# A decoder step on one core: the down projection in 47 passes instead of 40, with its operands made over three units

## Chip, core and metric

The kernel runs on one core of one Trainium2 chip. The metric is device time in microseconds of a whole execution; lower is better. A profiled execution also has a span, from its first to its last instruction.

## What is computed

One layer of a hybrid decoder on 512 prompt tokens and 8 x 8 sample tokens, 576 tokens in all, in float32: a mixer (gated linear attention and a state-space branch with a shared input and output projection), and behind it a feed-forward part. The change is in the latter:

```
def _conv_ffn(xn, s_ffn, p):
    u = xn @ p['ffn_w_in']                                  # 2048 -> 2 x 5632
    u, buf = _causal_dwconv(u, s_ffn, p['ffn_conv_w'], p['ffn_conv_b'])
    a, b = jnp.split(u, 2, axis=-1)
    return (jax.nn.silu(a) * b) @ p['ffn_w_out'], buf       # 5632 -> 2048
# in _layer:
x = x + _rmsnorm(f, p['n_ffn_post'])
```

## The kernel before, in words

Activations lie with channels on the 128 partitions and the 576 tokens along the free axis, in two halves of 288. A float32 product is made of three matmuls: operands are split into a high part (ScalarE copies to the rounded type) and a low part (VectorE subtracts), and high x high, high x low and low x high are added in PSUM (`three`, L1880 to L1882). On top of that, most of the feed-forward part multiplies 2 x 2 blocks by a scheme with seven products in place of eight, so sums of weight blocks and sums of activation blocks are needed, each split in two as well.

**Units.** The matrix work is an ordered stream of units. A unit is one block of 512 KB of weights (`raw`, two buffers, loaded by SP in order) and, in the down projection, two steps of seven products of three matmuls, 42 matmuls. Units are counted here from the start of the down projection: unit 0 is the loop's w = WUNITS (160), unit -1 the last of the up projection; a group of four up units gives one pair of tiles of gate input. For each unit ScalarE makes the high parts (`hi_a` L1069, `hi_s` L1079) and VectorE the sums (L2502, L2509, L2516) and the low parts (`direct_lows` L2527, `sum_lows` L2534). ScalarE may start on a unit two ahead of TensorE; the operand ring has three slots.

**The down projection.** K, the 44 gate tiles g (5632 channels), is cut into 21 pairs of tiles and two tiles for a tail. Each pair kp is loaded back from DRAM (`g_spill`) by SP (`kp_load` L573), VectorE forms its four sums in three steps (`g_first`, `g_second`, `g_third`: L2749, L2756, L2763), ScalarE makes the high parts of all seven (`g_highs` L1205, 128x2016), VectorE the low parts (`g_lows` L2769, 128x2016). There are five slots for pairs (G_SLOTS), so a pair can be loaded only when the pair five before has had its last use (`freed`, L511). The output is 8 pairs of tiles j. WINDOWS (L78) cuts the 21 pairs of each j into windows, and a pass (r, j) is window r of output pair j: in it TensorE accumulates seven products in seven of the eight PSUM banks over its steps. The 40 passes have 168 steps in 84 units. The passes of round 0 are copied to the arena by ScalarE (`take_pass` L1213, L1225). The later ones, except the last two, are staged: ScalarE copies each bank to the one buffer `m_stage`, and POOL adds it to the arena by two accumulating DMAs (L668), of products 0 to 3 and 4 to 6; the next staged pass waits for each half's DMA before it is copied. TensorE's next pass may use bank q + 1 only when product q of the last pass has been copied. The last two passes are added from PSUM by VectorE (L2786).

**The order on each engine** is fixed by one loop over w (ScalarE L1292, VectorE L2884, SP L589). `g_made_at` (L519) gives the unit in whose iteration a pair is made, with sums, high parts and low parts in the same iteration; `combined_at` (L523) the iteration in which the seven products of an output pair are combined to tiles (`combine` L2788, L2797 to L2804). SP loads a pair when its slot's last unit is done, three iterations behind in its own order, ahead of the next raw block in the same queue; `h_load` (L585) brings the residual back in the same way (10 tiles, then 6).

**The end.** A tail of 32 tile halves of six matmuls (`last_down` L1948) adds the last two tiles of K, VectorE takes them (`take_last` L2925), ScalarE squares them, the sums of squares go through TensorE (L1980, L1988), and VectorE and POOL scale (`y_of` L2931), add the residual and give the rows to the output DMAs.

The core of what sets the order, before:

```
WINDOWS = ((2, 5, 5, 5, 4),) * 4 + ((3, 5, 5, 5, 3),) * 2 + ((4, 5, 5, 4, 3), (5, 5, 5, 3, 3))
g_made_at = {WUNITS - 2: 0, WUNITS - 1: 1, WUNITS + 2: 2, WUNITS + 5: 3, WUNITS + 7: 4}
for _kp in range(5, DOWN_KP):
    g_made_at[max(freed(_kp) + 2, max(g_made_at) + 1)] = _kp
```

This puts pairs 0 to 20 in units -2, -1, 2, 5, 7, 11, 12, 21, 26, 28, 31, 32, 41, 46, 48, 51, 52, 61, 66, 68 and 70.

## Time and profile before

| | |
|---|---|
| median of 3 runs | 2566.02 us (2564.46 to 2573.86) |
| the profiled execution's own time | 2566.72 us |
| its span | 2564.9 us |
| TensorE matmuls, busy | 2462.2 us, 96% of the span |
| VectorE, busy | 1837.9 us, 72% |
| ScalarE, busy | 1080.8 us, 42% |
| POOL, busy | 444.8 us, 17% |
| mean granted TensorE clock | 0.983 |
| the chain that ended last, by engine | TensorE 76%, VectorE 11%, DMA 5%, ScalarE 4% |

Busy times are of the span. The execution's own time lies 1.8 us above its span, and 0.7 us above the median of the three runs. Matmuls overlap in the pipeline, so a matmul's duration in a row is longer than the time from one to the next; the latter is what a stretch costs. The granted clock is a share of TensorE's 2.4 GHz: 1.00 is that level and 0.50 is 1.2 GHz, and a stretch in between had some time at each. "issue" as a releaser means that the profile shows nothing that the instruction waited for.

### The profile page before, as it was taken

What the parts mean: (1) busy time and instruction counts of PE and PEld (TensorE: products, weight loads), DVE (VectorE), ACT (ScalarE), POOL (GpSimd) and SP (SyncE); (2) the same over time, 40 slices, a digit from 0 to 9 for tenths busy, and PEclk for the clock granted to TensorE, in tenths of its full rate; (3) what the DMA queues carried; (4) which work ended last, traced back from release to release, by engine and by line L of the source; (5) the groups of instructions that cost most, each with busy time, mean ns of one, the idle gap of its engine ahead of it and who ended that gap; (6) DMA issues with size and microseconds to landing.
All of it is one profiled execution on the core that took longest, in us unless ns stands there. A gap on an engine that the chain in (4) does not pass through costs nothing.

```text
span 2564.9 us, 48674 instructions
## 1 busy us (share of the span) xinstructions
PE 2462.2 (96%) x20078; PEld 2423.8 (94%) x20078; DVE 1837.9 (72%) x2763; ACT 1080.8 (42%) x1653; POOL 444.8 (17%) x268
## 2 busy tenths in 40 slices
PE   7999999999999999999999999999999899999986
PEld 7999999999999999899999999999998898989986
DVE  6543555755236368898888888988888767676778
ACT  5332222433213245444444444444445545545542
POOL 3333223433233361000000000000000011111115
PEclk9999999999999999999999999999999999999998
DMA  5223237622472424233333333333334367676883
GB/s 178 83 82 96 77 121 260 211 75 72 136 255 82 156 68 143 86 112 107 108 108 111 107 111 113 112 103 106 111 106 145 102 159 184 162 184 157 200 209 119
DMA packets 106284, 334.29 MB, mean 130 GB/s; under 512 B 11344, under 2 KB 16080, under 8 KB 105184
## 3 DMA queue, kind: packets, MB, share of 16 engines
q1 hardware_dynamic: 66400, 229.53, 28.1%
q10 hardware_dynamic: 31040, 70.90, 7.7%
q0 software_dynamic: 8640, 30.97, 6.7%
q8 instruction: 149, 2.44, 0.4%
q14 instruction: 55, 0.45, 0.1%
HBM read 255.77 MB, written 44.62 MB: 117 GB/s over the span
## 4 chain that ended last, share of the span: by engine, by line
PE 76%; DVE 11%; DMA 5%; ACT 4%; issue 3%; SPq 0%; POOL 0%; ACTq 0%; DVEq 0%
PE psum_proj L1379 18%; PE psum_proj L1381 9%; PE psum_proj L1880 7%; PE psum_proj L1882 7%; PE psum_proj L1881 7%; PE psum_work L1880 7%; PE psum_work L1882 7%; PE psum_work L1881 7%; DMA raw<-in_weights_dram 4%; PE psum_work L1379 1%; ACT ops_a L1205 1%; DVE w_lo L2534 1%; DVE w_lo L2527 1%; PE psum_work L1381 1%; DVE arena L2450 1%
## 5 line engine op out<-in xcount | busy, mean ns | idle before, releaser
L1379 PE MATMUL psum_proj<-x_hi,w_hi 128*128 128x288 f32 (+2 forms) x1696 | 510.9, 301 | 15.0 <-DVE x_lo L2031 12.9
L1379 PE MATMUL psum_proj<-x_lo,w_hi 128*128 128x288 f32 (+2 forms) x1696 | 501.2, 296 | 0.0
L1381 PE MATMUL psum_proj<-x_hi,w_lo 128*128 128x288 f32 (+2 forms) x1696 | 500.8, 295 | 0.0
L613 POOL TENSOR_TENSOR w_lo<-raw,w_hi 128x1024 fp32r<-128x1024 f32 x128 | 321.7, 2515 | 619.6 <-ACT w_hi L707 619.6
L707 ACT ACTIVATE w_hi<-raw 128x1024 fp32r<-128x1024 f32 x138 | 145.3, 1056 | 486.5 <-PE psum_proj L1381 412.0
L1379 PEld LDWEIGHTS psum_proj<-x_hi,w_hi 128*128 128x128 f32 x1696 | 320.7, 189 | 22.2 <-issue 15.4
L1379 PEld LDWEIGHTS psum_proj<-x_lo,w_hi 128*128 128x128 f32 x1696 | 320.0, 189 | 2.7 <-issue 1.9
L1381 PEld LDWEIGHTS psum_proj<-x_hi,w_lo 128*128 128x128 f32 x1696 | 319.7, 188 | 0.0
L668 POOL DMA_DIRECT2D arena<-m_stage x60 | 51.9, 868 | 1456.8 <-ACT m_stage L1225 1455.0
L1880 PE MATMUL psum_proj<-ops_a,w_hi 128*128 128x288 f32 x808 | 245.3, 304 | 29.9 <-issue 10.6
L1880 PE MATMUL psum_work<-ops_a,w_hi 128*128 128x288 f32 x782 | 234.8, 300 | 16.7 <-issue 13.0
L1882 PE MATMUL psum_proj<-ops_a,w_lo 128*128 128x288 f32 x808 | 242.3, 300 | 0.0
L1882 PE MATMUL psum_work<-ops_a,w_lo 128*128 128x288 f32 x782 | 233.6, 299 | 0.0
L1881 PE MATMUL psum_proj<-ops_a,w_hi 128*128 128x288 f32 x738 | 221.9, 301 | 0.0
L1881 PE MATMUL psum_work<-ops_a,w_hi 128*128 128x288 f32 x712 | 213.4, 300 | 0.0
L1077 ACT ACTIVATE w_hi<-raw 128x768 fp32r<-128x768 f32 x162 | 136.9, 845 | 141.0 <-PE psum_work L1882 60.3
L1880 PEld LDWEIGHTS psum_proj<-ops_a,w_hi 128*128 128x128 f32 x808 | 156.0, 193 | 35.1 <-issue 15.9
L1880 PEld LDWEIGHTS psum_work<-ops_a,w_hi 128*128 128x128 f32 x782 | 150.5, 192 | 18.4 <-issue 13.8
L2527 DVE TENSOR_TENSOR w_lo<-raw,w_hi 128x768 fp32r<-128x768 f32 x162 | 154.6, 954 | 15.5 <-ACT w_hi L1077 15.4
L1882 PEld LDWEIGHTS psum_proj<-ops_a,w_lo 128*128 128x128 f32 x808 | 156.4, 194 | 0.0
L1082 ACT ACTIVATE w_hi<-tail 128x1024 fp32r<-128x1024 f32 x81 | 86.1, 1063 | 156.5 <-DVE tail L2516 156.5
L1882 PEld LDWEIGHTS psum_work<-ops_a,w_lo 128*128 128x128 f32 x782 | 150.7, 193 | 0.0
(452 smaller groups left out, 6786.6 us busy)
## 6 DMA issues: line engine op xcount, KB each, us to landing
raw<-in_weights_dram SPq DMA_DIRECT2D x386, 512.0 KB, 3.6
arena<-m_stage POOLq DMA_DIRECT2D x30, 576.0 KB, 5.2
arena<-m_stage POOLq DMA_DIRECT2D x30, 432.0 KB, 7.2
g_spill<-x_flat ACTq DMA_DIRECT2D x44, 288.0 KB, 2.1
x_flat<-g_spill SPq DMA_DIRECT2D x18, 576.0 KB, 5.1
spill<-tail ACTq DMA_DIRECT2D x24, 288.0 KB, 2.1
arena<-in_xT_dram SPq DMA_DIRECT2D x4, 1152.0 KB, 10.6
y_spill<-arena ACTq DMA_DIRECT2D x4, 1152.0 KB, 4.9
```

Of the source, the lines that this page charges most:

```text
L613: nc.gpsimd.tensor_tensor(w_lo[:, slot], raw[:, r], w_hi[:, slot].bitcast(F32), ALU.subtract).then_inc(lo_ready, 1)
L668: pool.dma_start(m_of(j, first, stop), m_stage[:, first * HALF:stop * HALF], accum_op=ALU.add)\
L707: nc.scalar.activation(w_hi[:, slot], raw[:, r], ACT.Copy).then_inc(hi_ready, 1)
L1077: nc.scalar.activation(w_slot(w, 0)[:, 0:6], raw[:, w % 2, 2:8], ACT.Copy).then_inc(hi_ready, 1)
L1082: nc.scalar.activation(w_slot(w, 0)[:, 6:14], w_sums[w % 2], ACT.Copy).then_inc(whs_ready, 1)
L1205: nc.scalar.activation(g_high_part(kp), g_sums(kp), ACT.Copy).then_inc(op_high, 1)
L1379: nc.tensor.matmul(banks[:, n, 0:b - a], w_hi[:, slot, k], (hi, lo)[part][:, a:b], start=first and part == 0, stop=False)
L1381: mm = nc.tensor.matmul(banks[:, n, 0:b - a], w_lo[:, slot, k], hi[:, a:b], start=False, stop=last)
L1880: nc.tensor.matmul(to, w_h, hi, start=first, stop=False)
L1881: nc.tensor.matmul(to, w_h, lo, start=False, stop=False)
L1882: return nc.tensor.matmul(to, w_l, hi, start=False, stop=last)
L2527: tt_op(w_slot(w, 1)[:, 0:6], raw[:, w % 2, 2:8], w_slot(w, 0)[:, 0:6].bitcast(F32), ALU.subtract)\
```

## The change

The windows of the eight output pairs are cut anew, into 47 passes of at most five steps (six rounds; output pair 7 ends in round 4), so the last uses of the k pairs are spread over the units. Round 0 still has 8 passes; 37 passes are staged in place of 30. The 168 steps and 84 units stay. The passes of output pair 7 are over early, and its two tiles (14, 15) are the first of the tail (LAST_TILES); the combining of output pairs 4, 5 and 6 stands in the tail in place of 6 and 7.

Making a pair is spread over three iterations: sums and high parts in iteration `made`, the low parts in two instructions (4/7 and 3/7 of the columns) in the next two, each behind the lows of the unit's own weights. Pairs 0 to 20 now have their sums in units -8, -2, 3, 6, 9, 12, 15, 18, 21, 25, 31, 37, 40, 43, 46, 49, 55, 60, 63, 66 and 69. Pair 0's sums are formed in `m_stage`, which is not used before round 1; its high parts come in unit -4 and its low parts in -3 and -2; pair 1 has both low parts in -1, pair 2 both in 4. The residual's load moves from iteration 79 to 78 and the tail tiles' load from 72 to 73.

```diff
@@ -75,8 +75,10 @@
 
 
 DOWN_KP, DOWN_PAIRS = FT // 2 - 1, KT // 2
-WINDOWS = ((2, 5, 5, 5, 4),) * 4 + ((3, 5, 5, 5, 3),) * 2 + ((4, 5, 5, 4, 3), (5, 5, 5, 3, 3))
-PASSES = [(r, j, sum(WINDOWS[j][:r]), sum(WINDOWS[j][:r + 1])) for r in range(5) for j in range(DOWN_PAIRS)]
+WINDOWS = ((2, 3, 4, 3, 5, 4), (2, 3, 5, 3, 4, 4), (2, 3, 4, 5, 4, 3), (2, 4, 4, 5, 3, 3), (3, 4, 4, 4, 3, 3),
+           (3, 3, 5, 4, 3, 3), (4, 4, 3, 5, 3, 2), (4, 4, 4, 4, 5))
+PASSES = [(r, j, sum(WINDOWS[j][:r]), sum(WINDOWS[j][:r + 1])) for r in range(6) for j in range(DOWN_PAIRS)
+          if r < len(WINDOWS[j])]
 STEPS = [(p, kp) for p, (r, j, first, stop) in enumerate(PASSES) for kp in range(first, stop)]
 FIRST_STEP = [sum(q < p for q, kp in STEPS) for p in range(len(PASSES))]
 END_STEP = [sum(q <= p for q, kp in STEPS) - 1 for p in range(len(PASSES))]
@@ -87,6 +89,9 @@
 TAIL_UNITS = 4
 UNITS = TAIL_UNIT0 + TAIL_UNITS
 G_SLOTS = 5
+
+LAST_PASS = [max(p for p, (r, i, first, stop) in enumerate(PASSES) if i == j) for j in range(DOWN_PAIRS)]
+LAST_TILES = (14, 15) + tuple(range(14))
 
 BY_VE = (len(PASSES) - 2, len(PASSES) - 1)
 STAGED = [p for p, (r, j, first, stop) in enumerate(PASSES) if r and p not in BY_VE]
@@ -363,7 +368,7 @@
         def g_sums(kp):
 
             at = 4032 * (kp % G_SLOTS) + 2016
-            return smalls[:, 0:2016] if kp % G_SLOTS == 4 else XF[:, at:at + 2016]
+            return m_stage[:] if kp == 0 else smalls[:, 0:2016] if kp % G_SLOTS == 4 else XF[:, at:at + 2016]
 
         def g_tail(q, low):
 
@@ -375,8 +380,8 @@
         h_in = XF[:, 6336:6336 + KT * T].rearrange("p (n t) -> p n t", n=KT)
         H_FIRST = 10
 
-        fsum, fsum_v = A(0, 576), A(2016, 576)
-        fsq = [A(2016 * (2 + i), 576) for i in range(4)]
+        fsum, fsum_v = A(2016 * 7, 576), A(0, 576)
+        fsq = [A(2016 * (1 + i), 576) for i in range(3)] + [w_sum_b[:, 0:576]]
 
 
         const_in = sem("const_in")
@@ -510,18 +515,26 @@
 
         def freed(kp):
 
+            if kp == 0:
+                return WUNITS - 14
             if kp < 4:
                 return WUNITS - 4 + kp // 2
             if kp == 4:
                 return WUNITS + 2
             return WUNITS + LAST_USE[kp - G_SLOTS] // 2
 
-        g_made_at = {WUNITS - 2: 0, WUNITS - 1: 1, WUNITS + 2: 2, WUNITS + 5: 3, WUNITS + 7: 4}
+        made = [WUNITS - 8, WUNITS - 2, WUNITS + 3, WUNITS + 6, WUNITS + 9]
         for _kp in range(5, DOWN_KP):
-            g_made_at[max(freed(_kp) + 2, max(g_made_at) + 1)] = _kp
+            made.append(max(freed(_kp) + 2, made[-1] + 3))
+        g_made_at = {w: kp for kp, w in enumerate(made)}
+        g_high_at = {(w if kp else WUNITS - 4): kp for kp, w in enumerate(made)}
+        g_low_at = {WUNITS - 3: ((0, 0),), WUNITS - 2: ((0, 1),), WUNITS - 1: ((1, 0), (1, 1))}
+        g_low_at[made[2] + 1] = ((2, 0), (2, 1))
+        for _kp in range(3, DOWN_KP):
+            for _half in range(2):
+                g_low_at[made[_kp] + 1 + _half] = ((_kp, _half),)
         TAIL_FREED, H_FREED = (WUNITS + LAST_USE[kp] // 2 for kp in (16, 17))
-        combined_at = {WUNITS + END_STEP[p] // 2 + 2: j for p, (r, j, first, stop) in enumerate(PASSES)
-                       if r == 4 and p not in BY_VE}
+        combined_at = {WUNITS + END_STEP[p] // 2 + 3: j for j, p in enumerate(LAST_PASS) if p not in BY_VE}
 
         L = BATCHES - LATE_B
 
@@ -680,8 +693,8 @@
             def add_h(n, kt):
 
                 pool.wait_ge(y_m, KT * n + kt + 1)
-                a = cut(acc(kt), n)
-                nc.gpsimd.tensor_tensor(a, a, cut(h_in[:, kt ^ 1], n), ALU.add).then_inc(added_p, 1)
+                a = cut(acc(LAST_TILES[kt]), n)
+                nc.gpsimd.tensor_tensor(a, a, cut(h_in[:, LAST_TILES[kt] ^ 1], n), ALU.add).then_inc(added_p, 1)
 
             for kt in POOL_SUMS:
                 square_sum(0, kt)
@@ -1202,6 +1215,8 @@
             def g_highs(kp):
 
                 act.wait_ge(op_sum, KP + kp + 1)
+                if kp == 0:
+                    act.wait_ge(units_done, DOWN_UNIT0 - 3)
                 nc.scalar.activation(g_high_part(kp), g_sums(kp), ACT.Copy).then_inc(op_high, 1)
 
             def g_tail_highs():
@@ -1220,8 +1235,8 @@
                     else:
                         to = m_stage[:, M_AT[q] * HALF:(M_AT[q] + 1) * HALF]
                         before = STAGED.index(p)
-                        if before and q in (0, M_SPLIT):
-                            act.wait_ge(m_acc[q // M_SPLIT], 16 * before)
+                        if q in (0, M_SPLIT):
+                            act.wait_ge(*((m_acc[q // M_SPLIT], 16 * before) if before else (op_low, G_OPS0 + 1)))
                     nc.scalar.activation(to, bank(7 * p + q), ACT.Copy).then_inc(part_out, 1)
 
             def hi_tail(v):
@@ -1317,8 +1332,8 @@
                     g_out(g - 1)
                 if step + 1 in END_STEP and END_STEP.index(step + 1) not in BY_VE:
                     take_pass(END_STEP.index(step + 1))
-                if w in g_made_at:
-                    g_highs(g_made_at[w])
+                if w in g_high_at:
+                    g_highs(g_high_at[w])
                 if w == TAIL_FREED + 3:
                     g_tail_highs()
                 if w >= ALL_UNITS - 2:
@@ -1341,7 +1356,7 @@
                         act.wait_ge(ysq_sum, len(POOL_SUMS) * n + POOL_SUMS.index(max(kt - 4, 1)) + 1)
                     elif kt > 4:
                         act.wait_ge(ysq_vsum, len(VE_SUMS) * n + VE_SUMS.index(max(kt - 4, 5)) + 1)
-                    nc.scalar.activation(cut(fsq[kt % 4], n), cut(acc(kt), n), ACT.Square).then_inc(squared, 1)
+                    nc.scalar.activation(cut(fsq[kt % 4], n), cut(acc(LAST_TILES[kt]), n), ACT.Square).then_inc(squared, 1)
                     if n and kt == 2:
                         act.wait_ge(fo_st, 16)
                         root_of_tokens(0)
@@ -1352,8 +1367,8 @@
                 by_ve = sum(kt < stop for kt in VE_ADDS[n])
                 act.wait_ge(added_v, len(VE_ADDS[0]) * n + by_ve)
                 act.wait_ge(added_p, 2 * KT + (KT - len(VE_ADDS[0])) * n + stop - by_ve)
-                i, a = divmod(first, 4)
-                act.dma_start(yT[i, :, a:a + 2, n * HALF:(n + 1) * HALF], acc_rows(first, n)).then_inc(y_st, 16)
+                i, a = divmod(LAST_TILES[first], 4)
+                act.dma_start(yT[i, :, a:a + 2, n * HALF:(n + 1) * HALF], acc_rows(LAST_TILES[first], n)).then_inc(y_st, 16)
 
             for n in range(2):
                 for first in range(0, KT, 2):
@@ -2762,11 +2777,14 @@
                 ve.wait_ge(own_step, second_step)
                 tt_op(f[G4], f[G21], f[G2], ALU.add).then_inc(op_sum, 1)
 
-            def g_lows(kp):
+            def g_lows(kp, half):
 
                 ve.wait_ge(op_high, G_OPS0 + kp + 1)
                 ve.wait_ge(op_sum, KP + kp + 1)
-                tt_op(g_low_part(kp), g_sums(kp), g_high_part(kp).bitcast(F32), ALU.subtract).then_inc(op_low, 1)
+                a, z = ((0, 4 * HALF), (4 * HALF, 7 * HALF))[half]
+                low = tt_op(g_low_part(kp)[:, a:z], g_sums(kp)[:, a:z], g_high_part(kp)[:, a:z].bitcast(F32), ALU.subtract)
+                if half:
+                    low.then_inc(op_low, 1)
 
             def g_tail_lows():
 
@@ -2787,7 +2805,7 @@
 
             def combine(j):
 
-                p = 4 * DOWN_PAIRS + j
+                p = LAST_PASS[j]
                 m = m_of(j).rearrange("p (n t) -> p n t", n=7)
                 if p in BY_VE:
                     ve.wait_ge(*product_out(p, 6))
@@ -2893,6 +2911,8 @@
                     take_pass(END_STEP.index(step))
                 if w + 1 < ALL_UNITS:
                     sum_lows(w + 1)
+                for low_kp, half in g_low_at.get(w, ()):
+                    g_lows(low_kp, half)
                 if kp is not None:
                     g_first_step = g_first(kp)
                 if w + 2 < ALL_UNITS:
@@ -2911,21 +2931,20 @@
                     gate_product(g - 1)
                 if u == 3 and w < WUNITS:
                     evacuate(g)
+                if step + 1 in END_STEP[:-1] and END_STEP.index(step + 1) in BY_VE:
+                    take_pass(END_STEP.index(step + 1))
                 if w in combined_at:
                     combine(combined_at[w])
-                if kp is not None:
-                    g_lows(kp)
                 if w == TAIL_FREED + 3:
                     g_tail_lows()
                 if w >= ALL_UNITS - 2:
                     tail_lows(w - ALL_UNITS + 2)
-            combine(6)
             take_pass(BY_VE[1])
 
             def take_last(e):
 
                 ve.wait_ge(tile_mm, LAST_MM0 + e + 1)
-                a = cut(acc(e % KT), e // KT)
+                a = cut(acc(LAST_TILES[e % KT]), e // KT)
                 tt_op(a, last_bank(e), a, ALU.add).then_inc(taken, 1)
 
             def y_of(n, kt):
@@ -2934,11 +2953,11 @@
                     ve.wait_ge(ysq_mm, 2 * n + 2)
                     ve.wait_ge(h_back, 32)
                     ve.wait_ge(squared, Y_SQUARES0 + KT * (n + 1))
-                a = cut(acc(kt), n)
-                stt(a, a, V("ffn_post", kt), work[:, n, 0:HALF], ALU.mult, ALU.mult).then_inc(y_m, 1)
+                a, d = cut(acc(LAST_TILES[kt]), n), LAST_TILES[kt]
+                stt(a, a, V("ffn_post", d), work[:, n, 0:HALF], ALU.mult, ALU.mult).then_inc(y_m, 1)
                 if kt in VE_ADDS[n]:
                     ve.wait_ge(y_m, KT * n + kt + 1)
-                    tt_op(a, a, cut(h_in[:, kt ^ 1], n), ALU.add).then_inc(added_v, 1)
+                    tt_op(a, a, cut(h_in[:, d ^ 1], n), ALU.add).then_inc(added_v, 1)
 
             def square_sum(n, kt):
 
@@ -2952,10 +2971,10 @@
             settle()
             for e in range(2 * KT):
                 take_last(e)
-                if e in (1, 5):
-                    tail_lows(2 + e // 4)
-                if e == 3:
-                    combine(7)
+                if e in (1, 6):
+                    tail_lows(2 + e // 5)
+                if e in (3, 5, 8):
+                    combine((4, 5, 6)[e // 3 - (e == 3)])
                     settle()
                 n, kt = divmod(e - 1, KT)
                 if kt in VE_SUMS:
@@ -2996,7 +3015,7 @@
     down = f_out.reshape(FT, P, KT, P).transpose(2, 0, 1, 3)
     blocks = [[down[2 * PASSES[p][1] + n, 2 * kp + 1 - o] for o, n in ((0, 1), (0, 0), (1, 0), (1, 1))] for p, kp in STEPS]
     blocks = np.array(blocks).reshape(DOWN_UNITS, 2, 4, P, P).transpose(0, 3, 2, 1, 4).reshape(-1, P, 8, P)
-    tail = down[:, 2 * DOWN_KP:].reshape(-1, 8, P, P).transpose(0, 2, 1, 3)
+    tail = down[list(LAST_TILES), 2 * DOWN_KP:].reshape(-1, 8, P, P).transpose(0, 2, 1, 3)
 
     out = w_out.reshape(2, 8, P, KT, P).transpose(0, 3, 2, 1, 4)[::-1]
     out = np.concatenate([out[:, 8:], out[:, :8]], axis=1).reshape(-1, P, 8, P)
```

## Rows read from the trace of the kernel before

**Rows 1.** Stretches: us, then busy PE, PEld, DVE, ACT, POOL; clock, DMA share, GB/s

```profile
1959.70:2507.70 548.00, 494.30 (x3528) 487.31 (x3529) 389.39 (x556) 274.62 (x462) 51.88 (x60) 0.95 0.63 165
1959.70:1978.20 18.50, 12.84 (x64) 11.94 (x65) 18.29 (x31) 9.45 (x17) 0.00 (x0) 0.72 0.25 79
2048.90:2065.60 16.70, 11.19 (x66) 10.74 (x65) 13.90 (x18) 5.80 (x9) 0.00 (x0) 0.80 0.23 64
2065.60:2141.10 75.50, 75.50 (x568) 75.30 (x568) 49.09 (x71) 40.48 (x69) 10.51 (x12) 1.00 0.73 184
...
2176.80:2192.00 15.20, 11.15 (x65) 10.72 (x65) 12.26 (x18) 5.40 (x8) 0.00 (x0) 0.78 0.31 82
...
2462.20:2482.70 20.50, 10.65 (x65) 10.21 (x64) 10.18 (x17) 7.57 (x17) 2.34 (x3) 0.75 0.81 256
...
2507.70:2564.90 57.20, 37.17 (x254) 35.04 (x252) 46.98 (x104) 17.39 (x39) 34.78 (x40) 0.81 0.38 128
```

**Rows 2.** TensorE's waits, 1950 to 2565 us: total, times, longest

```profile
PE psum_proj L1880 <- DVE ops_a L2769: 12.3, 4, 3.8
```

**Rows 3.** TensorE in order of time: start, us, what [idle before <-releaser]

```profile
1962.80 0.37 PE L1880 MATMUL psum_proj<-ops_a,w_hi 128*128 128x288 f32 x1 [3.14 <-DVE w_lo L2534]
...
2053.54 0.37 PE L1880 MATMUL psum_proj<-ops_a,w_hi 128*128 128x288 f32 x1 [1.71 <-issue]
...
2060.35 0.61 PE L1880 MATMUL psum_proj<-ops_a,w_hi 128*128 128x288 f32 x1 [3.80 <-DVE ops_a L2769]
```

**Rows 4.** VectorE in order of time, two units that each make a pair

```profile
2048.57 2.26 DVE L2769 TENSOR_TENSOR ops_a<-x_flat,ops_a 128x2016 fp32r<-128x2016 f32 x1 [2.54 <-ACT ops_a L1205]
2050.74 0.95 DVE L2527 TENSOR_TENSOR w_lo<-raw,w_hi 128x768 fp32r<-128x768 f32 x1
...
2053.35 0.75 DVE L2749 TENSOR_TENSOR x_flat<-x_flat 128x576 f32<-128x576 f32 x1
2054.02 0.42 DVE L2509 TENSOR_TENSOR tail<-tail,raw 128x256 f32<-128x256 f32 x1
2054.35 0.45 DVE L2756 TENSOR_TENSOR x_flat<-x_flat 128x288 f32<-128x288 f32 x1
...
2058.04 2.26 DVE L2769 TENSOR_TENSOR ops_a<-x_flat,ops_a 128x2016 fp32r<-128x2016 f32 x1 [2.53 <-ACT ops_a L1205]
```

**Rows 5.** VectorE in order of time, the last up units and unit 0

```profile
1935.54 0.46 DVE L2696 TENSOR_TENSOR x_flat<-psum_proj,smalls 128x288 f32<-128x288 f32 x1 [1.78 <-ACT smalls L1155]
...
1950.86 0.69 DVE L2502 TENSOR_TENSOR tail<-raw 128x512 f32<-128x512 f32 x1 [1.74 <-DMA raw<-in_weights_dram]
...
1957.83 2.26 DVE L2769 TENSOR_TENSOR ops_a<-x_flat,ops_a 128x2016 fp32r<-128x2016 f32 x1 [2.32 <-ACT ops_a L1205]
...
1964.69 0.45 DVE L2696 TENSOR_TENSOR x_flat<-psum_proj,smalls 128x288 f32<-128x288 f32 x1
```

**Rows 6.** DMA queues and issues, 2040 to 2520 us: share; KB, us to landing

```profile
q0 software_dynamic: 8640, 30.97, 36.0%
q1 hardware_dynamic: 16956, 52.84, 31.9%
...
arena<-m_stage POOLq DMA_DIRECT2D x30, 432.0 KB, 7.2
...
x_flat<-h_spill SPq DMA_DIRECT2D x1, 2880.0 KB, 15.7
```

**Rows 7.** ScalarE's waits, 1960 to 2520 us: total, times, longest

```profile
ACT m_stage L1225 <- DMA arena<-m_stage: 0.4, 1, 0.4
```

**Rows 8.** The accumulating DMAs of L668, all 60

```profile
DMA to landing us min/median/max: 4.8/6.1/11.5
```

**Rows 9.** VectorE in order of time, behind the residual's load

```profile
2476.14 0.69 DVE L2502 TENSOR_TENSOR tail<-raw 128x512 f32<-128x512 f32 x1 [10.14 <-DMA raw<-in_weights_dram]
```

**Rows 10.** VectorE in order of time, behind the loop

```profile
2506.51 0.75 DVE L2797 TENSOR_TENSOR arena<-arena 128x576 f32<-128x576 f32 x1
...
2509.33 0.81 DVE L2786 TENSOR_TENSOR arena<-psum_proj,arena 128x288 f32<-128x288 f32 x2
```

## The prediction

> **What bounds the kernel now.** The page comes first: TensorE is busy nearly throughout, and the chain that ended last runs mostly through it, so the question is where TensorE loses time in the stage that the change touches. The table by stretch answers it [rows 1]. In the stall-free stretch of 75.5 us 568 matmuls ran, 0.133 us each at a granted clock of 1.00. The down projection, from 1959.7 to 2507.7 us, has 84 units of 42 matmuls, the 3528 that its row counts; at 0.133 they need 469 us, and it took 548. So 79 us are lost there at a mean clock of 0.95: 54 as idle time (548.0 less the 494.3 that it was busy) and the rest as matmuls at the 1.2 GHz level after idle time.
>
> The table of waits and TensorE's gaps in order of time say where [rows 2, 3]. Three gaps of 3.8 us (one stands in the rows, the others are at 2187 and 2313 us) are put down to the low parts of a k pair (VectorE, L2769), each behind a unit that began with a gap with no releaser ("issue", as before 2053.54 us). VectorE's order of work shows why [rows 4]. A unit's own operands cost it 3.3 us. A k pair adds its sums, 1.4 us, and the low parts, 2.17 us from start to start, but between the two VectorE waits 2.53 us for ScalarE's high parts, which come only when the sums are there. From one low part to the next, in two units that both make a pair, pass 9.47 us, where TensorE uses 5.58 a unit. One such unit eats the lead that VectorE has; two in a row stop TensorE twice. Late sums also hold ScalarE in its queue, so the eviction of a finished pass starts late, and TensorE stops before the next pass's second product.
>
> By loss (stretch less matmuls x 0.133): the start 10 us (18.5 less 64); pairs 5 and 6, the first double make, 7.9 us (16.7 less 66), pairs 10 and 11 6.6 (15.2 less 65), pairs 15 and 16 about as much, 20.7 together; the load of the residual 11.9 us (20.5 less 65) [rows 1]; 36.5 us are left for the single makes and late evictions.
>
> **The parts of the change.**
> *Operands over three units, makes at least three units apart.* A make unit now costs VectorE 3.3 + 1.4 = 4.7 us, the next 3.3 + 1.3, the third 3.3 + 1.0: 13.7 us (with 0.1 for a second instruction) against 3 x 5.58 = 16.7. The 2.53 us wait goes, unless ScalarE sits in the eviction of a pass; it then ends about 2.3 us into the next unit, where VectorE still has some 3 us of lead. The three double makes and the single ones should stop stalling: 20.7 + 36.5 us at most. I keep 6 us back for pairs whose first use is one unit after the last low part, or in that unit (2, 3, 4, 13, 14, 20; for pair 3 I get 0.5 us to spare), and 2 us for units 37, 46 and 55, where a make, a late weight load and a pass with an odd last step meet. **Gain 49 us.**
>
> *First pair early.* Pair 0's sums go to unit -8, its high parts to -4, the low parts to -3 and -2; pair 1 is formed at -2 and finished at -1 behind the unit's own lows. Now VectorE waits until 1957.83 us, splits pair 0 until 1960.0, and only then makes unit 0's lows; TensorE gets them at 1962.80 after 3.14 us, and the last up tile is taken at 1964.69 [rows 3, 5]. After, unit 0's lows can be done by 1958.3, before TensorE asks at 1959.7, pair 1's lows by 1960.6, and the tile is taken from about 1961.5: TensorE waits 1.5 us at its third product and follows the takes. The 10 us become 4. What is moved costs 1.4 us in group -8 and 2.2 us in -3 and -2, covered by VectorE's waits in those groups, 1.78 us for part 0's copy and 1.74 us for raw weights [rows 5]; the second wait shrinks with only one pair's load ahead of it, and that pays for it. Without the cover it would cost 2 us. **Gain 6 us.**
>
> *47 passes.* TensorE's matmuls stay 3528. Seven more staged passes are 49 more evictions on ScalarE, which is busy for 274.6 of the 548 us [rows 1] and does them beside TensorE, and 14 more accumulating DMAs on POOL's queue. Their queue held the 16 engines for 36.0% of 480 us, 173 us or 5.8 a pass; the loads took 31.9%, 153 us [rows 6]. After, it is 37 x 5.8 + 153 = 368 us against 72 units x 5.58 = 402 of TensorE: 92% full where before it was 68%. With passes of three steps (8.4 us, 13 of them behind a staged pass) a half must land before the next pass is evicted: landing of the second half 7.2 after its issue [rows 6] and 1.2 for the last evictions is 8.4, with 1.5 us of slack by the spare PSUM bank; under load it is more. I take 4 us: the trace of before shows one such wait, 0.4 us [rows 7], but it has few passes so short. Bounds: 0, if the landing stays; and 80 if it is always the longest, 11.5 [rows 8] (the rival below); I stay near the lower end, by the row of 0.4. **Cost 4 us.**
>
> The Trainium skill ("DMA: Bandwidth & Descriptors", section "Anatomy of one DMA — SWDGE (gpsimd) path") prices such a DMA at about 2.0 us plus its bytes at 436 GB/s, by which a pass would hold the engines for an estimated 2.4 us, leave them near half empty, and make the 4 us zero. The measured 5.8 us decides.
>
> *The residual's load* keeps its form: 2880 KB, 15.7 us to landing [rows 6], go ahead of the raw weights in SP's queue, now before unit 78 instead of 79, and VectorE waited 10.14 us for those weights [rows 9]. I leave its 11.9 us; bounds 9 and 15, as more accumulations share the engines.
>
> *The end.* Passes 45 and 46 are taken by VectorE. Before, the combining of two pairs of tiles stood behind the loop (2.8 us, from 2506.51 to 2509.33 [rows 10]), now that of three (4, 5, 6), while the last pass is taken some 1.7 us earlier. VectorE is busy for 47.0 of the last 57.2 us, TensorE for 37.2 [rows 1], so one more combining of 2.8 us, less what the earlier take gives back, plus the order of tiles: **cost 3.5 us**, bounds 0 (if TensorE's later gaps cover it) and 5.
>
> **Sum.** 49 + 6 - 4 - 3.5 = 47.5 us off the profiled execution's 2566.72 gives 2519; its median twin is 2566.02, 0.7 lower, so **2518.5 us**.
>
> **Rivals.**
> *The DMA engines become the bound* (faster, but by half). For it: 92% full, and in the stretches of three-step passes with a pair's load 5.8 + 1.5 x 1.5 + 1.7 = 9.8 us of transfers stand against 8.4 of TensorE. Raw weights then land late for every unit. Against: in the stall-free stretch they were 73% busy [rows 1] without harm, and the two raw buffers allow a landing of 7.4 us (two units, 11.2, less 3.8 of issue and VectorE's work between). Price: 1.4 us in each of 13 short passes and a raw landing too late at the 16 pair loads by 0.5 is 26 us, of which 4 are counted: about 2541. The Trainium skill ("DMA: Bandwidth & Descriptors", section "Queues, rings and completion order") says that an engine serves its queues in turn by packets: a raw load is then slowed beside an accumulation and not held behind it. That bears on how late, not on whether, and no row of before isolates it.
>
> *Deadlines too near.* Pairs 2, 3, 4, 13, 14 and 20 miss their first use as the double makes do now, a gap of 3.8 and 2.5 at the slow clock each: 6 x 6.3 less the 6 kept back = 32 us worse: 2550. For it: the slack is one unit or none. Against: VectorE's lead in quiet stretches is more than a unit.
>
> *Slower: the one stage buffer.* ScalarE may not evict a pass until the halves of the last one have landed. If the second half lands in 11.5 us throughout, a cycle is 12.7 us: 13 three-step passes lose 4.3 each and 16 of four steps 1.5 each, 80 us, and ScalarE, stuck there, delays the weight sums too. This passes the gain from a landing of about 10.5 us on (before: median 6.1 over both halves [rows 8]), and would give 2566 - 51.5 + 80 = 2594.
>
> *It does not do what it says*: the stalls come from the weights alone, and the makes only coincide: within 10 us of 2566. Against: the gaps end with L2769 [rows 3] and VectorE waits before it for ScalarE alone [rows 4].
>
> **How the numbers follow.** Forecast 0.64 (own range 2506 to 2532), DMA bound 0.18 (2532 to 2550), deadlines 0.09, stage buffer 0.04, no effect 0.05. 0.5% is 12.8 us, about what a measurement here can tell: the limit is 2553. Faster: 0.64 + 0.18 + 0.07 (most of the deadlines' case) = 0.89, plus 0.02 of the last two cases: 0.91. Slower 0.03, same 0.06. The low end takes every bound at its best (evictions and end at 0, 5 of the 8 us kept back, and 3 at the residual's load), 2503; the high end reaches through the DMA case, 2543.
>
> **What would show it.** Right: no gap put down to L2769; VectorE's idle time before it small; 84 units in about 492 us; the granted clock of that stretch 0.98 or more; TensorE's first product of the down projection without a wait for L2534; one long gap, about 9 us, at unit 78; DMA share near 0.75 over the stage. Wrong: gaps released by ScalarE's m_stage copies that themselves waited for the accumulating DMA (stage buffer), waits of VectorE for raw weights in most units with gaps marked "issue" (DMA bound), gaps at pairs 2, 3, 4 (deadlines). If the stretch from the last down unit to the end grows by more than 5 us, the price of the end was wrong.

## The result, and the profile after

The changed kernel takes **2550.71 us** (median of 9 runs, 2546.99 to 2558.79) against 2570.03 for the kernel before in the same job (9 runs, 2564.46 to 2573.86): ratio 0.9926, 95% interval 0.9913 to 0.9938. It is faster by 19 us, where 47.5 were forecast, and it lies 8 us above the end of the range. The profiled execution took 2550.71 us, span 2548.9.

The same stretches in the changed kernel's trace (columns as in [rows 1]): the down projection, its first 17 us, the place of unit 38, and the tail.

```profile
1957.01:2484.75 527.74, 488.19 (x3529) 480.58 (x3528) 378.29 (x562) 291.21 (x511) 63.93 (x74) 0.97 0.73 184
1957.01:1974.20 17.19, 14.74 (x95) 13.81 (x94) 16.95 (x30) 10.64 (x24) 0.00 (x0) 0.90 0.35 121
2176.80:2192.00 15.20, 11.31 (x69) 10.87 (x68) 7.34 (x11) 6.50 (x11) 1.72 (x2) 0.82 0.69 208
...
2484.75:2548.90 64.15, 38.01 (x260) 35.64 (x258) 53.44 (x111) 17.17 (x39) 34.10 (x40) 0.84 0.35 118
```

The down projection went from 548.0 us to 527.7, where the forecast's own terms give 497 (548 - 49 - 6 + 4; its list of signs says 492), and the tail from 57.2 to 64.2. The up projection ends 2.7 us earlier in this execution, which belongs to neither and is likely of this execution: in three of the kernels below that share this up projection the down projection starts at 1959.0, 1960.4 and 1961.3 us, against 1957.0 here and 1959.7 before.

Waits of the changed kernel from 1957 to 2549 us (total, times, longest), TensorE's, then ScalarE's, then VectorE's:

```profile
PE psum_proj L1895 <- ACT m_stage L1240: 12.7, 9, 2.4
PE psum_work L1895 <- ACT m_stage L1240: 10.6, 10, 2.4
PE psum_work L1895 <- issue: 10.1, 2, 9.5
...
PE psum_proj L1895 <- issue: 3.2, 2, 1.7
...
ACT w_hi L1090 <- DMA raw<-in_weights_dram: 74.2, 17, 12.5
...
ACT m_stage L1240 <- DMA arena<-m_stage: 10.3, 8, 2.1
...
DVE w_sum_b L2517 <- DMA raw<-in_weights_dram: 97.3, 21, 14.8
DVE tail L2517 <- DMA raw<-in_weights_dram: 32.9, 11, 5.9
DVE ops_a L2785 <- ACT ops_a L1220: 6.9, 4, 2.6
```

What stands in the place of the last line in the kernel before, 1957 to 2565 us:

```profile
DVE ops_a L2769 <- ACT ops_a L1205: 45.3, 16, 5.6
```

[Rows 2] has no line of its kind any more: TensorE waits nowhere for the low parts of a pair, and VectorE's waits for ScalarE's high parts, the longest item of its list before, are short. In their place stand 23.3 us of gaps, 19 of them, each ended by ScalarE's copy of a finished pass into the stage buffer (L1240), and the waits for raw weights about doubled: VectorE's from 71 to 130 us, ScalarE's (L1090; L1077 before) from 43 to 88. ScalarE also waits for the accumulating DMAs before it may refill the stage buffer, 10.3 us in 8 waits where [rows 7] had 0.4 in one.

The DMA part of the trace, 2040 to 2500 us, as in [rows 6]:

```profile
q0 software_dynamic: 10422, 37.29, 46.5%
q1 hardware_dynamic: 16471, 51.09, 30.8%
...
raw<-in_weights_dram SPq DMA_DIRECT2D x70, 512.0 KB, 6.0
arena<-m_stage POOLq DMA_DIRECT2D x36, 576.0 KB, 5.5
arena<-m_stage POOLq DMA_DIRECT2D x36, 432.0 KB, 7.9
x_flat<-g_spill SPq DMA_DIRECT2D x12, 576.0 KB, 7.1
```

The accumulations' share rose from 36.0% to 46.5%. Their own landing hardly moved (432 KB: 7.2 to 7.9 us), but a load of raw weights now takes 6.0 us to land at the median, where it took 4.1 before in the same window.

How a late load reaches TensorE shows at unit 38. In order of time: the issues of SyncE (SP), then VectorE, ScalarE and TensorE.

```profile
2164.51 0.33 SPq L606 DMA_DIRECT2D raw<-in_weights_dram  x1
2171.99 0.38 SPq L595 DMA_DIRECT2D x_flat<-g_spill  x1
2172.49 2.14 SPq L606 DMA_DIRECT2D raw<-in_weights_dram  x1
2177.56 0.38 SPq L595 DMA_DIRECT2D x_flat<-g_spill  x1
...
2170.67 0.95 DVE L2542 TENSOR_TENSOR w_lo<-raw,w_hi 128x768 fp32r<-128x768 f32 x1
...
2182.64 0.69 DVE L2517 TENSOR_TENSOR w_sum_b<-raw 128x512 f32<-128x512 f32 x1 [7.61 <-DMA raw<-in_weights_dram]
2183.26 1.22 DVE L2549 TENSOR_TENSOR w_third<-tail,w_third 128x1024 fp32r<-128x1024 f32 x1
...
2186.22 1.06 ACT L1095 ACTIVATE w_hi<-w_sum_b 128x1024 fp32r<-128x1024 f32 x1 [2.73 <-DVE w_sum_b L2531]
2187.18 0.39 ACT L1240 ACTIVATE m_stage<-psum_proj 128x288 f32<-128x288 f32 x1
...
2184.58 0.37 PE L1895 MATMUL psum_proj<-ops_a,w_third 128*128 128x288 f32 x1 [1.47 <-issue]
...
2187.62 0.61 PE L1895 MATMUL psum_proj<-ops_a,w_third 128*128 128x288 f32 x1 [2.42 <-ACT m_stage L1240]
```

SyncE's program issues in order. It issued a raw load at 2164.51 and then stood 7.1 us in the next pair's load (L595, which waits for TensorE to leave the slot) until 2171.99; the raw load behind it, of unit 39's block, went out at 2172.49. Not all of these 7.1 us are lost to that load: its buffer was in use until VectorE had read it, at 2171.62 (2170.67 + 0.95), so it went out 0.87 us later than it could have. What the order did as well is to put the pair's 576 KB ahead of it in the same DMA queue. POOL had just issued two accumulations (2170.47 on, 1008 KB together), the pair's load has 576 KB and the raw load 512: about 2.1 MB in flight at once. The raw load landed 10.1 us after its issue. The queues' shares of the 16 engines in the first 4.2 us of these (2172.5 to 2176.7):

```profile
q0 software_dynamic: 186, 0.70, 96.4%
q1 hardware_dynamic: 37, 0.09, 5.9%
```

The accumulations (q0) had the engines nearly to themselves, and the two loads (q1) moved most of their bytes after that. Until the raw load was there, at 2182.64, VectorE and ScalarE both stood idle. Everything queued on them came late: VectorE's low parts of the unit that TensorE was about to start (2183.26; the gap of 1.47), then the next unit's sums, ScalarE's high parts of them (2186.22), and behind those in ScalarE's queue the eviction of the pass that had ended (2187.18; the gap of 2.42). TensorE's following matmuls run 0.44 us instead of 0.29, at a granted clock of 0.50 (2187.7 to 2191.5), the 1.2 GHz level.

Counted in the same trace over units 5 to 79: 17 raw loads stood right behind a pair's or the tail tiles' load. They went out 0.0 to 3.9 us after their buffer was free, 1.7 on average and 30 us in all, and landed 7.8 us after their issue at the median, 10.4 at most. The other raw loads went out at once and landed in 4.5 us at the median.

### The profile page after: what moved, and what is told of

The parts are those of the page before. It is cut to its first block, busy times and chain, and to the rows that moved or that the text cites. A ratio compares the mean times of both kernels' runs of the same rounds, so it can differ in the third digit from the quotient of the medians.

```text
span 2548.9 us, 48805 instructions
## 1 busy us (share of the span) xinstructions
PE 2452.7 (96%) x20078; PEld 2414.3 (95%) x20078; DVE 1838.4 (72%) x2784; ACT 1098.2 (43%) x1702; POOL 455.7 (18%) x282
## 4 chain that ended last, share of the span: by engine, by line
PE 78%; DVE 9%; DMA 8%; issue 3%; ACT 2%; SPq 0%; ACTq 0%; POOL 0%; DVEq 0%
PE psum_proj L1394 18%; PE psum_proj L1396 9%; PE psum_proj L1895 7%; PE psum_proj L1897 7%; PE psum_proj L1896 7%; PE psum_work L1895 7%; PE psum_work L1897 7%; PE psum_work L1896 7%; DMA raw<-in_weights_dram 6%; PE psum_work L1394 1%; DMA arena<-m_stage 1%; PE psum_work L1396 1%; DVE w_lo L2549 1%; DMA out_ssd_s_dram<-arena 1%; DVE arena L2465 1%
## 5 line engine op out<-in xcount | busy, mean ns | idle before, releaser
L681 POOL DMA_DIRECT2D arena<-m_stage x74 | 63.9, 866 | 1428.7 <-ACT m_stage L1240 1427.1
L1895 PE MATMUL psum_proj<-ops_a,w_hi 128*128 128x288 f32 x808 | 241.3, 299 | 17.1 <-ACT m_stage L1240 5.2
L1896 PE MATMUL psum_proj<-ops_a,w_hi 128*128 128x288 f32 x742 | 220.5, 297 | 0.0
L1090 ACT ACTIVATE w_hi<-raw 128x768 fp32r<-128x768 f32 x162 | 136.6, 843 | 151.2 <-DMA raw<-in_weights_dram 74.2
L2517 DVE TENSOR_TENSOR w_sum_b<-raw 128x512 f32<-128x512 f32 x122 | 84.0, 688 | 97.3 <-DMA raw<-in_weights_dram 97.3
```

The source lines that it names most:

```text
L681: pool.dma_start(m_of(j, first, stop), m_stage[:, first * HALF:stop * HALF], accum_op=ALU.add)\
L1090: nc.scalar.activation(w_slot(w, 0)[:, 0:6], raw[:, w % 2, 2:8], ACT.Copy).then_inc(hi_ready, 1)
L1895: nc.tensor.matmul(to, w_h, hi, start=first, stop=False)
L1896: nc.tensor.matmul(to, w_h, lo, start=False, stop=False)
L2517: own(tt_op(s[:, 0:2], r[:, 1:4:2], r[:, 0:1].broadcast_to([P, 2, 2 * P]), ALU.add))
```

## The experiments

Three questions: what the order of SyncE's queue costs, what the accumulated bytes cost, and what each part of the change is worth by itself. The kernel before measured 2568.6 us beside the first four runs and 2570.5 beside the others; differences under 3 us between runs of the first job and later ones are not read.

**Pair loads on ScalarE's queue** (from the changed kernel; pairs 5 to 20)

```diff
-                for kp in range(DOWN_KP):
+                for kp in range(G_SLOTS):
                     if freed(kp) + 3 == w:
                         kp_load(kp)
...
                 if more:
                     hi_a(w + 2)
+                for kp in range(G_SLOTS, DOWN_KP):
+                    if freed(kp) + 1 == w:
+                        kp_load(kp)
```

> The changed kernel with the loads of pairs 5 to 20 moved from SP's queue, where the next raw block stands behind each of them, to ScalarE's queue, issued one unit after the slot is free. Theory A (order: the raw block that stands in SP's queue behind the pair's load, and behind its wait for TensorE, comes late; ScalarE stands before that raw block in its own order and so evicts the finished pass late): ScalarE's waits for raw weights fall from 88 us to under 25, TensorE's waits for its m_stage copies from 23 us to under 8, and the kernel takes 2520 to 2530 us, against 2551 for the changed kernel. Theory B (bandwidth: seven more passes of accumulation slow every load): the landing of a raw block stays near the changed kernel's median of 6 us, the m_stage waits stay over 18 us, and the time is within 6 us of 2551. Theory C (ScalarE waits for the one stage buffer itself): as B.

2531.82 us (ratio 0.9855, 0.9834 to 0.9876): 19 us off the changed kernel. ScalarE's waits for raw weights fell from 88 to 42 us and TensorE's for the stage copies from 23.3 to 14.4:

```profile
PE psum_proj L1905 <- ACT m_stage L1247: 10.1, 6, 3.8
...
PE psum_work L1905 <- ACT m_stage L1247: 4.3, 4, 1.8
...
ACT w_hi L1090 <- DMA raw<-in_weights_dram: 32.4, 7, 12.7
...
ACT w_third L1090 <- DMA raw<-in_weights_dram: 9.7, 3, 5.3
```

The time is 2 us above the range expected of the queue's order, and the waits fell less than it said: the order is a cause. The wait of the pair's load now stands in ScalarE's program instead, and ScalarE's waits for TensorE before L1090 rose from 23 to 55 us; that this is why the gain is smaller than in the next run is likely and not shown.

**Pair loads one raw load later**, on SyncE's queue

```diff
-                    if freed(kp) + 3 == w:
+                    if freed(kp) + (4 if kp >= G_SLOTS else 3) == w:
                         kp_load(kp)
```

> The changed kernel with the loads of pairs 5 to 20 in SP's queue as before, but one raw block later in the order, so the raw block of unit freed + 4 goes out ahead of SP's wait and the load. Theory A: most of the gain of the move to the other queue, 2523 to 2540 us, with new waits of VectorE for the pair itself, some 2 to 4 us where a pair is made two units after its slot is free (9 of 16), which its lead should mostly cover. Theory B and C: within 6 us of 2551.

2525.83 us (0.9839, 0.9819 to 0.9859): 25 us from one moved line. SyncE's waits in the pair loads fell from 89 us to 25:

```profile
SPq L595 <- PE psum_work L1897: 13.1, 6, 3.2
SPq L595 <- PE psum_proj L1897: 11.7, 5, 3.4
```

and TensorE's for the stage copies from 23.3 to 7.5:

```profile
PE psum_proj L1895 <- ACT m_stage L1240: 6.4, 6, 2.0
...
PE psum_work L1895 <- ACT m_stage L1240: 1.1, 2, 0.7
```

The bytes and the seven extra passes are unchanged here (q0 holds the engines for 48.3%), so full engines alone do not cost those 25 us. Raw loads no longer go out late (5 us in all where it was 30), and only two of them still stand behind a pair's load. At the steps of units 38, 47 and 56 TensorE loses 2.3, 0.7 and 3.6 us; in the changed kernel it is 7.0, 3.5 and 7.2. Neither this run nor the last tells the late issue from the pair's bytes ahead of the raw load: both take both away.

**A quarter of the accumulated columns**

```diff
-                    pool.dma_start(m_of(j, first, stop), m_stage[:, first * HALF:stop * HALF], accum_op=ALU.add)\
-                        .then_inc(m_acc[half], 16)
+                    part = [v.rearrange("p (q t) -> p q t", t=HALF)[:, :, 0:HALF // 4]
+                            for v in (m_of(j, first, stop), m_stage[:, first * HALF:stop * HALF])]
+                    pool.dma_start(part[0], part[1], accum_op=ALU.add).then_inc(m_acc[half], 16)
```

> The changed kernel with each accumulating DMA over a quarter of the columns: three quarters of the staged partial sums are left out of the output, so these DMAs take a quarter of the bytes. Theory B: raw blocks land in about 4 us again, nearly all of the 43 us that TensorE loses around evictions goes, and the time is about 2512. Theory A: a raw block behind a pair still comes some 6 us after TensorE releases the slot, and half of the loss stays: 2525 to 2535. Theory C: ScalarE's waits for the accumulating DMA (10.3 us) go, and with them about 10 us: 2541.

2506.93 us (0.9756, 0.9734 to 0.9778), 44 us off the changed kernel, below what each theory gave. Three quarters of the staged partial sums are left out. The DMA part, 2040 to 2480 us:

```profile
q1 hardware_dynamic: 16494, 51.18, 36.3%
q0 software_dynamic: 33808, 9.40, 24.9%
raw<-in_weights_dram SPq DMA_DIRECT2D x71, 512.0 KB, 4.2
```

With the old order of the queue the stage-copy gaps are gone from TensorE's list, and so are ScalarE's waits for the accumulating DMAs. Yet the raw loads behind a pair's load still go out late, 48 us in all and so more than the changed kernel's 30; they land in 5.5 us at the median instead of 7.8. A late issue does little harm, then, where the load is quick; that is tested from the other side below.

**The same quarter with the pair loads one raw load later** (both edits above)

> The kernel with the pair loads one raw load later (2525.8 us), each accumulating DMA over a quarter of its columns; it leaves out three quarters of the staged partial sums. It tells whether the order of the queue and the bytes are one cause or two. Theory A (one cause: the order costs only because the bytes make each load slow; with a quarter of the bytes the order of the changed kernel already cost next to nothing): 2500 to 2507, at most 6 us under the quarter run with the old order (2506.9). Rival (two causes that add up, 24.9 us for the order and 43.8 us for the bytes): 2480 to 2486.

2504.15 us (0.9747, 0.9732 to 0.9763). By itself the order was worth 25 us and the bytes 44, together 47. **They overlap**: with a quarter of the bytes the order is worth some 3 us, hardly more than can be read between the two jobs, and not 25. So the order costs only where the loads are slow. The bytes are worth 44 us with the old order and still 22 (2525.8 to 2504.2) with the new one, so they have a cost of their own too. A raw load that is late in the queue *and* slow to land overruns the two raw buffers.

**The old windows with the low parts one unit later** (from the kernel before: the split alone, 40 passes)

```diff
+                if g_made_at.get(w - 1, 0) >= 2:
+                    g_lows(g_made_at[w - 1])
...
-                if kp is not None:
+                if kp is not None and kp < 2:
                     g_lows(kp)
```

> The kernel before, with its 40 passes and its make units, in which only the low parts of pairs 2 to 20 are made one unit later, behind the next unit's own low parts. It tells the making apart from the windows. If the wait of VectorE for ScalarE's high parts is the main loss of before: the gaps put down to the low parts vanish, TensorE loses some 30 us less in the down projection and the time is 2535 to 2545, better than the changed kernel, since no pass is added. If the even windows are needed (two makes in a row remain too much, or pairs 6, 11, 16 and 20, first used one and a half units after their sums, come late): 2555 to 2570.

2541.16 us (0.9892, 0.9868 to 0.9915). The split alone beats the full change by 10 us. The time is in the range that the first theory gave, but its sign did not come: the gaps at the low parts were to vanish, and TensorE still stands there where windows free pairs close together:

```profile
PE psum_proj L1880 <- DVE ops_a L2769: 14.1, 5, 3.7
```

**The new windows with the low parts in the unit of the sums** (from the changed kernel; the windows without the split for pairs 3 to 20)

```diff
-                for low_kp, half in g_low_at.get(w, ()):
-                    g_lows(low_kp, half)
+                if w < made[3]:
+                    for low_kp, half in g_low_at.get(w, ()):
+                        g_lows(low_kp, half)
...
                     combine(combined_at[w])
+                if kp is not None and kp > 2:
+                    g_lows(kp, 0)
+                    g_lows(kp, 1)
```

> The changed kernel (2550.7 us) with the low parts of pairs 3 to 20 made at the end of the unit that makes the sums, as in the kernel before; the new windows, their 47 passes and the evenly freed pairs stay. It prices the split by itself beside the new windows. Theory A (with late raw weights ScalarE's high part comes late, and VectorE would wait for it in the same unit, where nothing else can go on): TensorE waits 3 to 5 us more at each of the 18 makes that meets late weights, 15 to 35 us in all, time 2565 to 2585. Rival B (the time of the stretch is set by the DMA engines, so that a stall at a make only stands in for one at the weights): 2550 to 2558.

2576.36 us (1.0024, 1.0012 to 1.0036), 26 us above the changed kernel and slightly above the kernel before. VectorE's waits for the high parts are back:

```profile
DVE ops_a L2785 <- ACT ops_a L1220: 49.9, 15, 6.5
DVE ops_c L2785 <- ACT ops_a L1220: 12.5, 4, 4.6
```

TensorE has 13 gaps with no releaser ("issue", 31 us with the residual's 9.5). The longest of the others, 3.76 us, ends as the unit's own low parts are done, which stood behind the pair's on VectorE (2108.51 + 1.22 = 2109.73):

```profile
2104.80 2.33 DVE L2785 TENSOR_TENSOR ops_a<-x_flat,ops_a 128x1152 fp32r<-128x1152 f32 x2 [2.53 <-ACT ops_a L1220]
2107.04 0.95 DVE L2542 TENSOR_TENSOR w_third<-raw,w_third 128x768 fp32r<-128x768 f32 x1
...
2108.51 1.22 DVE L2549 TENSOR_TENSOR w_third<-w_sum_b,w_third 128x1024 fp32r<-128x1024 f32 x1
...
2109.83 0.58 PE L1895 MATMUL psum_proj<-ops_a,w_third 128*128 128x288 f32 x1 [3.76 <-issue]
```

The split is worth about the same in either set of windows: 27 us in the old (2541.2 against 2568.6 beside it) and 26 in the new.

**The first pair not early** (from the changed kernel; pairs 0 and 1 are made whole in units -2 and -1 as before)

```diff
-            return m_stage[:] if kp == 0 else smalls[:, 0:2016] if kp % G_SLOTS == 4 else XF[:, at:at + 2016]
+            return smalls[:, 0:2016] if kp % G_SLOTS == 4 else XF[:, at:at + 2016]
...
-            if kp == 0:
-                return WUNITS - 14
...
-        made = [WUNITS - 8, WUNITS - 2, WUNITS + 3, WUNITS + 6, WUNITS + 9]
+        made = [WUNITS - 2, WUNITS - 1, WUNITS + 3, WUNITS + 6, WUNITS + 9]
...
+                if kp is not None and kp < 2:
+                    g_lows(kp, 0)
+                    g_lows(kp, 1)
```

> The changed kernel (2550.7 us) with the first pair in its old buffer, loaded at its old place, and pairs 0 and 1 made whole in the last two units of the up projection, as before. It prices the third term. Theory A (VectorE's gap at the start of the down projection comes back, 10 us against 4 us): 2555 to 2558. Rival (the start lies before every stall at the weights; a few us later there let the weights catch up): 2549 to 2552.

2555.63 us (0.9943, 0.9929 to 0.9957): the early pair is worth 4.9 us by the medians. The interval overlaps the changed kernel's (0.9913 to 0.9938), so the size is rough; the gaps agree with the sign. TensorE's gaps at the start of the down projection in this kernel,

```profile
1964.26 0.37 PE L1891 MATMUL psum_proj<-ops_a,w_hi 128*128 128x288 f32 x1 [3.20 <-DVE w_lo L2545]
1966.65 0.61 PE L1891 MATMUL psum_proj<-ops_a,w_hi 128*128 128x288 f32 x1 [1.37 <-DVE x_flat L2707]
1971.60 0.61 PE L1891 MATMUL psum_proj<-ops_a,w_hi 128*128 128x288 f32 x1 [0.97 <-DVE ops_a L2781]
```

and in the changed one:

```profile
1960.02 0.40 PE L1895 MATMUL psum_proj<-ops_a,w_hi 128*128 128x288 f32 x1 [1.53 <-DVE x_flat L2711]
...
1968.35 0.40 PE L1895 MATMUL psum_proj<-ops_a,w_hi 128*128 128x288 f32 x1 [0.92 <-ACT arena L1240]
```

**The old windows with both remedies** (the split and the pair loads one raw load later; 40 passes)

> The kernel before with the low parts one unit later (2541.2 us) and the pair loads one raw load later as well: 40 passes with both remedies, against 47 passes with both (2525.8 us). Theory A (the order of the queue costs wherever a pair load waits for its slot; with 40 passes the engines are less full and it costs less): 2528 to 2536, TensorE still waiting 10 to 14 us for VectorE where the old windows free pairs close together. Rival B (the seven extra passes cost more, through the DMA engines, than the evenly freed pairs bring): under 2524. Rival C (without the extra passes the order of the queue costs nothing): 2539 to 2543.

2525.40 us (0.9821, 0.9807 to 0.9836), the same as 47 passes with both (2525.83), 3 us under the range expected. The moved line is worth 16 us with 40 passes and 25 with 47. TensorE still loses 9.4 us at the low parts:

```profile
PE psum_proj L1880 <- DVE ops_a L2769: 9.4, 5, 2.5
PE psum_work L1880 <- issue: 8.5, 1, 8.5
```

The expectation had 5 to 13 us for that line with 40 passes. It is worth more, though raw loads landed in 5.0 us at the median without it and in 4.3 with it. The kernel before has the same order in its queue; what the moved line alone would bring there was not run.

**The residual in five loads** (on the kernel with the pair loads one raw load later)

```diff
-                if w == H_FREED + 3:
+                if H_FREED + 3 <= w < H_FREED + 8:
                     sp.wait_ge(units_done, W_UNIT0 + H_FREED + 1)
-                    h_load(0, H_FIRST)
+                    h_load(2 * (w - H_FREED - 3), 2 * (w - H_FREED - 2))
...
-            pool.wait_ge(h_back, 32)
+            pool.wait_ge(h_back, 96)
...
-                    ve.wait_ge(h_back, 32)
+                    ve.wait_ge(h_back, 96)
```

> The kernel with the pair loads one raw load later (2525.8 us), and the residual's one load of 2.95 MB cut into five of 590 KB, one behind each of five raw loads. Theory A (the wait of 7.8 us near 2445 us is one raw load standing behind one long transfer in the queue's order; in small pieces each raw load is late by 2 us at most, which the two raw buffers take up): the gap falls below 2 us and the time by 5 to 9 us, to 2517 to 2521. Rival D (the DMA engines have no time left in this stretch, and the same bytes delay the same loads wherever they stand): the one gap falls apart into several that sum to 6 to 10 us, and the time stays at 2523 to 2528.

**2517.55 us** (0.9799, 0.9781 to 0.9816), the fastest here but for those that leave work out: 2.0% under the kernel before, 1.3% under the changed one. The gap of 7.8 us is gone from TensorE's list and no other of its size took its place; each piece lands in 6.6 us at the median. ScalarE's waits for the accumulating DMAs are 20.0 us here, against 10.3 in the changed kernel; what they cost was not tested by itself.

**All three on the old windows** (the split, the moved pair loads, five residual loads; 40 passes)

> The kernel before with the low parts one unit later, the pair loads one raw load later (2525.4 us with both) and the residual's one load cut into five. It is the candidate with 40 passes beside the one with 47 (2517.6 us). Theory A (the wait of 8.5 us in TensorE's list is the residual alone and goes as it did with 47 passes): 2515 to 2519. If 40 passes leave the DMA engines more room, so that the pieces cost nothing at all, 2513 to 2515. Rival (the gap comes from another transfer in this schedule): 2523 to 2527.

2521.85 us (0.9811, 0.9796 to 0.9826), above the range that was expected and 4.3 us above the same remedies on 47 passes. The intervals of the two ratios overlap, so the sign of that difference is likely and not sure.

**The last combines two tiles later** (on the kernel with the pair loads one raw load later)

```diff
-                if e in (1, 6):
-                    tail_lows(2 + e // 5)
-                if e in (3, 5, 8):
-                    combine((4, 5, 6)[e // 3 - (e == 3)])
+                if e in (1, 3):
+                    tail_lows(2 + e // 3)
+                if e in (5, 7, 9):
+                    combine((4, 5, 6)[(e - 5) // 2])
```

> The kernel with the pair loads one raw load later (2525.8 us), and in the tail VectorE makes the last two low parts behind the last products 1 and 3 instead of 1 and 6, and combines pairs 4, 5 and 6 behind 5, 7 and 9 instead of 3, 5 and 8. Theory T (the tail grew from 57.2 to 64.1 us because the last low part, for which TensorE waits 3.43 us at 2502, stands behind two combines of 3 us each): that wait goes, TensorE's gap before the last sums of squares stays, and the time falls by 2 to 4 us, to 2522 to 2524. Rival U (three combines of 9 us in all lie on VectorE whatever their order, and VectorE carries the tail): the wait turns up before a later tile, and the time stays within 1 us of 2526.

2527.55 us (0.9831, 0.9815 to 0.9846), no difference. The wait for the last low part went and came back before a later tile:

```profile
PE psum_proj L1895 <- DVE arena L2948: 3.2, 2, 3.1
```

**Two combines left out** (on the kernel with five residual loads; the last additions of two pairs' quadrants are missing from the output)

```diff
-                if e in (3, 5, 8):
-                    combine((4, 5, 6)[e // 3 - (e == 3)])
+                if e == 3:
+                    combine(4)
```

> The kernel with five residual loads (2517.6 us) without the combines of pairs 5 and 6 in the tail; it leaves the last additions of the quadrants of these two pairs out. It prices VectorE's share of the tail's growth by 6.9 us. Theory U (VectorE carries the tail's first half, each combine there is worth its 3 us, and the wait of 3.4 us for the last low part goes as well): time down by 4 to 6 us, to 2512 to 2514. Rival V (TensorE's tail follows its own matmuls and the squares behind them; the combines lie in VectorE's idle time but for the one wait): down by 0 to 3 us, 2515 to 2518.

2514.22 us (0.9791, 0.9775 to 0.9807), 3.3 us less, between the two theories' ranges. In the traces the time from the tail's first gap to its last, before the last sums of squares, is 2493.84 - 2450.63 = 43.2 us with three combines and 2493.63 - 2455.22 = 38.4 with one: 1.7 to 2.4 us for each, of its 3 on VectorE.

## Why the prediction was wrong in size

The profiled execution came down by 16.0 us where the sum had 47.5, a miss of 31.5. By stretches, from the changed kernel's trace (the up projection came out 2.7 us shorter, which no term had):

*Start*: 17.19 us less 94 matmuls x 0.133 leaves 4.7 us of the former 10, predicted 4. The run without the early pair gives 4.9 us for the term, predicted 6. **Right.**

*Residual's load*: one gap of 9.5 us at unit 78 as forecast, 12.3 us lost over units 78 to 80, predicted 11.9. **Right**, and by the five-piece run 8 us of it could be had.

*The rest of the down projection*: 527.7 - 469.2 - 4.7 - 12.3 = 41.5 us, where the terms left 12 (the 8 kept back and 4 for the passes). **This is the miss, 29.5 us**, and two steps made it.

The first is "**47 passes, cost 4 us**". It was priced by one row, ScalarE's wait of 0.4 us for an accumulation [rows 7], as if the passes' only victim were the next pass. That wait did grow, to 10.3 us, but the accumulations' own landing changed little (median 6.7 us over all, from 6.1 [rows 8]), and with the pair loads moved the wait grew further, to 15.6 us, while the time fell by 25. So the rival of the stage buffer is wrong, and so is its price of 80 us. The main victims are the loads beside them: raw loads land in 6.0 us instead of 4.1. The fullness of 92% was worked out and put into the rival of the DMA engines, but at 26 us with a chance of 0.18; of that rival's two signs one came, VectorE's waits for raw weights, in 32 units. Gaps marked "issue" hardly did (3.8 us beside the residual's 9.5): the gaps end with the stage copies, which stand behind the late weights in ScalarE's queue. Its upper end, 2550, is where the kernel is. But it is not the full engines that hold the kernel there, since they are as full in the run that is 25 us faster. Of what the late loads cost, the rival's price had the slow landing (0.5 us over a limit of 7.4 at the pair loads; measured 7.8 at the median) and not that these loads also go out late, 1.7 us on average.

The second is "**2 us for units 37, 46 and 55, where a make, a late weight load and a pass with an odd last step meet**". At the steps behind these coincidences (units 38, 47 and 56) TensorE lost 7.0, 3.5 and 7.2 us over the length of its steps, 18 in all; with the pair loads one raw load later it is 6.5. The step counted VectorE's work in those units and left out what stands in the queues. An edit that evens out when pairs are freed also moves the pair loads, and each stands in SyncE's queue ahead of a raw load, waiting for TensorE and then landing first. The runs price that order, beside 47 passes, at 25 us, more than any part of the change but the split. How the 25 divide between the late issue and the bytes ahead stays open.

*The split itself*: forecast at 49 us for the operands over three units and the even windows together; the split measured 27 in the old windows and 26 in the new. In place of the prediction's one sum the runs give, by each one's ratio to the kernel before beside it: split -28 us, new windows with seven more passes and the new end +13, first pair -4, together -19. So the windows and passes, which were to be part of a gain, cost some 13 us, of which the end has a part; windows and passes were never run apart. With the loads reordered, the two sets of windows give the same time. The mechanism for VectorE was right: no gap is put down to a pair's low parts.

*The end*: 6.9 us more, predicted 3.5 and at most 5. **Mis-sized.** The first take in the tail is late by 2.69 us where it was 1.15, and from there to the last gap pass 42.2 us instead of 36.5. The prediction took the earlier end of the last pass as time given back; TensorE's first tile waits for just that pass. One more combine explains about 2 us of the 6.9 by the run that leaves two out; the rest was not taken apart.

*The other rivals.* Deadlines too near: no gap at pairs 2, 3 and 4 has the mark it was to have, wrong. No effect: the chain VectorE, ScalarE, VectorE was real (the run with the split undone is 26 us slower), wrong. On the sign the prediction was right. Of its signs, the wait for the unit's low parts at the first product is gone and the DMA share is 0.73, as it said; the stage's granted clock is 0.97 where it had 0.98 or more.

The Trainium skill ("DMA: Bandwidth & Descriptors", section "Queues, rings and completion order") says that an engine serves its queues in turn by packets. The trace of after agrees in part. At unit 38 the loads' queue moved 0.09 MB in the first 4.2 us beside two accumulations, with 5.9% of the engines' time, and 0.84 MB in the next 3.6 us (60.9%), before the second of them had landed. So the loads were not held until the accumulations were done, but for a while nearly so, which the prediction's "slowed and not held" did not reckon with.

## What to carry to other kernels

When a change moves where buffers are freed, write down for each in-order queue what now stands behind each wait, loads above all: here one kind of load moved behind the next was worth 25 us. Price added DMA traffic by what it does to the landing of the loads beside it and by how much lateness the buffers allow, not by its own waits. And try the parts of a change singly: the split alone beat the whole by 10 us.
